# RWKV scan with rate and write keys on 128 rows, and outputs one step behind

## What is computed

```python
def step(S, inp):
    r_t, w_t, k_t, v_t, kk_t, b_t = inp
    sa = jnp.einsum('bhvk,bhk->bhv', S, kk_t)
    S = S * w_t[:, :, None, :] - sa[..., None] * b_t[:, :, None, :] + v_t[..., None] * k_t[:, :, None, :]
    return S, jnp.einsum('bhvk,bhk->bhv', S, r_t)

xs = tuple(jnp.moveaxis(a, 1, 0) for a in (r, w, k, v, kk, b))
S, y = lax.scan(step, s0, xs, reverse=reverse)
```

## Time and profile before

| | us |
|---|---|
| median of 3 runs (lowest, highest) | 1204.44 (1199.67, 1204.90) |
| profiled execution | 1198.73 |
| its span in the trace | 1196.9 |
| PE busy | 1019.0 |
| DVE busy | 420.1 |
| ACT busy | 274.0 |
| POOL busy | 50.1 |
| first diagonal blocks of the scan to its last output | 427.2 to 654.05 |

### The profile page before, as it was taken

One profiled execution on the slowest core, in us unless ns is written; L12 is line 12 of the kernel. 1 busy time (PEld: TensorE's weight loads), 2 busy tenths in 40 slices (PEclk: granted clock), 3 DMA queues, 4 the chain that ended last, 5 costly groups with the idle time before them and its releaser, 6 DMA issues. The chain is left out here.

```text
span 1196.9 us, 22526 instructions
## 1 busy us (share of the span) xinstructions
PE 1019.0 (85%) x9838; PEld 620.8 (52%) x9838; DVE 420.1 (35%) x882; ACT 274.0 (23%) x538; POOL 50.1 (4%) x73
## 2 busy tenths in 40 slices
PE   3699999978777747988899999299999999999970
PEld 0265555544455547887898555244444444444430
DVE  1402642232488753372833664500000000010006
ACT  2311222223676511221122212011111111111101
POOL 0320000010000000000000000300000000000003
PEclk9899999988699877988989999589999999999995
DMA  9713342549998010102101821696899899898907
GB/s 345 236 23 140 120 162 87 196 152 406 407 404 350 10 29 3 39 12 74 47 14 56 316 71 41 239 342 241 318 343 348 306 352 345 311 352 321 331 35 263
DMA packets 95926, 244.95 MB, mean 205 GB/s; under 512 B 6612, under 2 KB 11508, under 8 KB 95328
## 3 DMA queue, kind: packets, MB, share of 16 engines
q1 hardware_dynamic: 85664, 218.64, 50.2%
q10 hardware_dynamic: 5824, 13.69, 2.9%
q0 software_dynamic: 4352, 11.34, 2.9%
HBM read 176.64 MB, written 67.01 MB: 204 GB/s over the span
## 5 line engine op out<-in xcount | busy, mean ns | idle before, releaser
L2091 PE MATMUL ps<-arena 128*128 128x512 f32 x544 | 239.9, 598 | 1.7 <-ACT arena L2141 1.7
L2091 PEld LDWEIGHTS ps<-arena 128*128 128x128 f32 x544 | 102.7, 191 | 127.1 <-issue 126.4
L2105 PE MATMUL ps<-arena 128*128 128x512 f32 x272 | 121.3, 599 | 3.6 <-ACT arena L2145 3.6
L696 PE MATMUL ps<-arena 128*128 128x512 f32 (+3 forms) x448 | 123.6, 435 | 0.0
L696 PEld LDWEIGHTS ps<-arena 128*128 128x128 f32 (+1 forms) x448 | 67.7, 188 | 60.2 <-issue 59.4
L2105 PEld LDWEIGHTS ps<-arena 128*128 128x128 f32 x272 | 50.6, 191 | 62.1 <-issue 62.1
L1760 PE MATMUL ps<-arena 128*128 128x512 f32 x160 | 70.6, 593 | 1.0 <-PEq L1237 1.0
L563 DVE SCALAR_TENSOR_TENSOR arena<-arena 128x128 f32<-128x128 f32 (+3 forms) x56 | 30.9, 552 | 82.6 <-ACT arena L440 81.1
L2182 DVE TENSOR_TENSOR arena<-arena,ps 128x512 f32<-128x512 f32 x17 | 11.7, 689 | 136.8 <-ACT arena L2137 136.8
L2190 DVE COPY arena<-ps 128x512 f32<-128x512 f32 x17 | 11.8, 693 | 125.9 <-PE ps L2105 125.9
L630 PE MATMUL ps<-arena 128*128 128x512 f32 (+1 forms) x160 | 52.4, 485 | 0.0
(11 more groups left out here) (307 smaller groups left out, 1385.3 us busy)
## 6 DMA issues: line engine op xcount, KB each, us to landing
gathered_tokens<-arena SPq DMA_DIRECT2D x16, 2560.0 KB, 26.0
arena<-in_exp_up_dram SPq DMA_DIRECT2D x17, 2048.0 KB, 18.2
arena<-in_exp_gate_dram SPq DMA_DIRECT2D x17, 2048.0 KB, 13.2
arena<-in_exp_down_dram SPq DMA_DIRECT2D x17, 2048.0 KB, 9.8
arena<-in_w_mod_dram SPq DMA_DIRECT2D x12, 2048.0 KB, 13.7
arena<-gathered_tokens SPq DMA_DIRECT2D x18, 512.0 KB, 15.1
expert_outputs<-arena ACTq DMA_DIRECT2D x17, 512.0 KB, 8.1
arena<-in_w_in_dram SPq DMA_DIRECT2D x4, 2048.0 KB, 7.8
```

The costliest lines, as they stand in the source:

```text
L696: mm = pe.matmul(ps[0:m, b, 0:hi - lo], ring[:, slot_of(what), k, (e % 4) * P:(e % 4) * P + m], hT[:, k, lo:hi], start=(k == 0), stop=(k = ...
L2091: mm = pe.matmul(ps[:, b, :], xgT[:, k, :], w[u][:, k, :], start=(k == 0), stop=(k == KT - 1))
L2105: mm = pe.matmul(ps[:, Y0 + half, :], hidT[:, k, :], wd[u][:, k, half * 512:(half + 1) * 512], start=(k == 0), stop=(k == 3))
```

## The change

Four things change in the scan.

First, the tile form. The pair of heads no longer gives the two halves of the rows of a tile; the direction or the kind of key does. A gram product takes the B and K keys of a head together as 128 stationary columns (for z = 1 in the order K, B, by place_of), and A and R as 128 moving ones, and writes 128 rows: one masked tile G takes the place of LR and MR, with one mask operation of 1024 columns per direction. turn_kb becomes 4 transposes per direction. UV holds for each direction the values in one half of the rows and the solved U in the other, so that one product over 128 rows does what two over 64 rows did; the state is kept as a block diagonal of 128 by 128 for each pair of heads. Right sides, solve products and outputs of both directions share one bank and one semaphore.

Second, the values. They are brought into UV by four DMAs a step on POOL's queue, and POOL clears the half in which U will stand, two steps ahead of use at the earliest (UV is double).

Third, the order. outputs(s) moves from behind new_states(s) to behind right_sides(s + 1). First visits of a chunk are copied to ytok by ScalarE, second ones added by VectorE.

Fourth, the output stage turns with 4 transposes of 128 columns where it had 16 products of 64.

The diff, cut:

```diff
+        def place_of(z, k):
+            return 5 - k if z and k >= B_ else k
...
+        G = [place_tile(2, 2 * NC4, 2 * C) for _ in range(2)]
+        KB = [place_tile(2, NC4, P) for _ in range(2)]
+        UV = [place_tile(2, NHEAD, C) for _ in range(2)]
...
+                for s in range(STEPS):
+                    if s >= 2:
+                        pool.wait_ge(y_mm, s - 1)
+                    u = UV[s % 2]
+                    for z in range(2):
+                        for p in range(2):
+                            pool.dma_start(rows(u, 1 - z)[:, z].rearrange("q (j p) n -> q j p n", p=2)[:, :, p, :],
+                                           rows(vt, p)[:, chunk_at(z, s)]).then_inc(ld_v[s % 2], 16)
+                    for z in range(2):
+                        if s or z:
+                            pool.wait_ge(u_zero, 2 * s + z)
+                        pool.memset(rows(u, z)[:, z], 0.0).then_inc(u_zero, 1)
...
+                def gram(s, z):
+                    for j in range(NC4):
+                        for p in range(2):
+                            mm = pe.matmul(ps[:, 2 * z + p, j * P:(j + 1) * P], both(rows(chm, p), z, s, j, B_), both(rows(chm, p), z, s, j, A_),
+                                           start=True, stop=True)
+                    mm.then_inc(g_mm[z], 1)
...
+                            mm = pe.transpose(ps[:, 2 * z, j * P:(j + 1) * P], both(chm, z, s, j, B_), ident)
...
+                    pe.wait_ge(ld_v[s % 2], 64 * (s // 2) + 64)
+                    pe.wait_ge(u_zero, 2 * s + 2)
+                    for j in range(NC4):
+                        if s:
+                            for z in range(2):
+                                pe.matmul(ps[64 * z:64 * z + 64, BRHS, j * P:(j + 1) * P], channels(A_, z, s, j), S[:, z, j],
+                                          start=True, stop=False)
+                        for p in range(2):
+                            for z in range(2):
+                                h = 2 * j + p
+                                mm = pe.matmul(ps[64 * z:64 * z + 64, BRHS, h * C:(h + 1) * C], G[s % 2][:, z, p * NC4 + j, 0:C], u[:, z, h],
+                                               start=(s == 0), stop=(s == 0 or p == 1))
...
+                            mm = pe.matmul(ps[:, BSN + z, j * P:(j + 1) * P], KB[s % 2][:, z, j], pair_of(UV[s % 2][:, z], j),
+                                           start=True, stop=True)
...
                     right_sides(s)
+                    if s:
+                        outputs(s - 1)
...
                         new_states(s)
-                    outputs(s)
-                    if more:
                         inverse(s + 1)
+                outputs(STEPS - 1)
...
+                def masked(s, z):
+                    dve.wait_ge(g_mm[z], s + 1)
+                    if s >= 2:
+                        dve.wait_ge(y_mm, s - 1)
+                    dve.tensor_tensor(G[s % 2][:, z], ps[:, 2 * z:2 * z + 2, :].rearrange("q b (j n) -> q (b j) n", j=NC4),
+                                      mask_s[:, z].unsqueeze(1).to_broadcast([P, 2 * NC4, 2 * C]), ALU.mult).then_inc(g_ok[z], 1)
...
-                for z in range(2):
-                    act.wait_ge(d2_mm[z], s + 1)
-                    act.activation(Uc[:, z], quarter(BSER + z), ACT.Copy).then_inc(uc_ok[z], 1)
+                    act.wait_ge(d2_mm, s + 1)
+                    act.activation(all_heads(rows(UV[s % 2], 0)[:, 0]), rows(ps, 0)[:, BRHS, :], ACT.Copy).then_inc(u_ok[0], 1)
...
+                    dve.wait_ge(d2_mm, s + 1)
+                    dve.tensor_copy(rows(UV[s % 2], 1)[:, 1], rows(ps, 1)[:, BRHS, :].rearrange("q (h n) -> q h n", n=C)).then_inc(u_ok[1], 1)
+                    if s:
+                        second_outputs(s - 1)
...
-                        for cc in range(2):
-                            for p in range(2):
-                                mm = pe.matmul(ps[64 * p:64 * p + 64, tt % 2, c4 * P + cc * C:c4 * P + (cc + 1) * C],
-                                               rows(yn[:, 2 * tt + cc, c4], p), rows(istack, p), start=True, stop=True)
+                        mm = pe.transpose(ps[:, tt % 2, c4 * P:(c4 + 1) * P], heads[:, c4 * P:(c4 + 1) * P], ident)
```

More of the change, by code:

```diff
@@ L82, in const_table @@
     near = ((s // 32 == t // 32) & (s // 16 != t // 16)).astype(np.float32)[:, None]
-    put("mask_b", np.stack([later * (cross - near), incl], 2))
-    put("mask_k", np.stack([later, incl], 2))
+    own = (half[:, None] == np.arange(2)[None])[:, :, None, None]
+    put("mask_s", np.where(own, np.stack([later * (cross - near), incl], 2), np.stack([later, incl], 2)))
     put("eye32", (q % 32)[:, None] == np.arange(32)[None])
@@ L1275, in diag_blocks @@
                     mm.then_inc(m_mm, 1)
-                def gram(s, k, bank, done):
-                    for z in range(2):
-                        for j in range(NC4):
-                            for p in range(2):
-                                q = 64 * half(z, p)
-                                mm = pe.matmul(ps[q:q + 64, bank + z, j * 2 * C:(j + 1) * 2 * C], kinds(k, z, s, j, p),
-                                               kinds(A_, z, s, j, p, 2), start=True, stop=True)
-                        mm.then_inc(done[z], 1)
+                def gram(s, z):
[4 more added lines that the diff above has]
+                    mm.then_inc(g_mm[z], 1)
@@ L1286, in turn_kb @@
                 def turn_kb(s):
                     for z in range(2):
[L1288 removed]
+                        pe.wait_ge(g_ok[z], s + 1)
                         for j in range(NC4):
[L1290 to L1294 removed]
@@ new lines, in right_sides, with by_inverse @@
+                    mm.then_inc(rhs_mm, 1)
+                def by_inverse(s, second, src, done):
+                    for j in range(NC4):
+                        for p in range(2):
+                            h = 2 * j + p
+                            for z in range(2):
+                                b = 1 - FIRST[z] if second else FIRST[z]
+                                q = 64 * z + 32 * b
+                                mm = pe.matmul(ps[q:q + 32, BRHS, h * C:(h + 1) * C], block32(XTf[s % 2], z, b)[:, p * NC4 + j],
+                                               block32(src, z, b)[:, h], start=True, stop=True)
+                    mm.then_inc(done, 1)
@@ L1400, in turned_states @@
+                    mm.then_inc(y_mm, 1)
+                def turned_states(bank, part_of, done):
                     for z in range(2):
```

406 lines of the change are left out of this document (196 added, 210 removed).

## The result

| | before | after |
|---|---|---|
| median (lowest, highest; 13 runs each, same chip) | 1202.78 (1197.22, 1210.96) | 1193.97 (1187.80, 1199.45) |
| profiled execution | 1198.73 | 1191.26 |
| its span in the trace | 1196.9 | 1189.5 |
| scan: first inverse copied out to the end of the last output | 457.52 to 654.05 = 196.5 | 460.30 to 649.28 = 189.0 |

The ratio of after to before is 0.9926, with a 95% interval of 0.9901 to 0.9951: the change gains 0.7%, some 9 us, where I had forecast 21. The time lies inside my wide range (1169 to 1202), 10 us above the forecast of 1184. The direction was right; the size was not.

The account below looks back on a forecast made before the run. TensorE's own instructions bound steady steps; clock loss, diagonal blocks, an issue gap and VectorE add elsewhere. Scan gain 19.0, less 0.5, plus 2.5 makes 21.0 us: from 1204.44 to 1183.4, forecast 1184, likely 1174 to 1190, wide range 1169 to 1202.

Parts of the forecast that it names:

- TensorE's own work in a step: Steady scan step: records times price per tile form sum to 12.6 us, 4.1 us a step less than before.
- step 9: Last scan step: two outputs in it and nothing to hide the copies, 11.6 to 11.9 us against 9.3, loss 2.6.
- the issue gap of step 4: Scan step 4: TensorE gaps of 3.4 and 1.1 us kept as before, in a step of 23.3 us.
- sign that I had named as proof against me: Scan: forecast wrong if PEclk is below 0.9 in steps 7 and 8, or steps 2 and 5 exceed 21 us.
- the first rival: Right sides and outputs: weight loads of column tiles follow one another, 0.7 us more each, 1197 us in all; chance 0.13.
- The waits: Steady step: inner products wait 0.6 us for VectorE's mask, next right sides 1.2 for its state update; step 14.45 us.
- a rival for the clock in steady steps: TensorE's clock falls in steps 2, 5, 7, 8 and 9 too, 10 us in all, 1194 us; chance 0.14.
- Steps 3 and 6: Scan: last row-solve piece, masks, products and update 19.1 us, about 2 of half clock: 21.1, gains 1.8 and 1.9.
- The values on POOL: Four DMAs and two memsets a step on POOL: 10.7 us against a need at 14.45, free with 3.7 to spare.
- The rival for slower: Right sides wait for POOL's value DMAs; at 10 us of landing 26 us more, 1209 us; chance 0.08.
- More is saved: Fewer records and denser tiles spare steps 1, 3, 4 and 6 their half clock: up to 1172 us; chance 0.10.
- Around the scan: Outside the scan: masks and copies before the solve lose 0.5 us, fewer transposes in the output stage gain 2.5.

Follow-up runs that it names:

- outputs_at_end: The changed kernel with each step's outputs put back behind its own new states and inverse; 1182.95 us, ratio 0.9849 to the kernel before.
- filled_last_step: outputs_at_end plus four unused 128x256 Matmuls in the waits of step 9; 1179.51 us, ratio 0.9791 to the kernel before.

## Why the prediction was right or wrong

The mechanism was right and sizes were off. Three terms of the sum failed: TensorE's own work in a step, put at 12.6 us and 13.9 in the trace; step 9, put at 11.9 and 17.2; and the issue gap of step 4, carried over from the kernel before, which grew from 3.4 to 6.4. Neither sign that I had named as proof against me came (PEclk is 1.00 in steps 7 and 8; steps 2 and 5 take 17.8 and 18.65 us). And errors cancelled: step 3 came 1.65 us over and step 2 1.9 under.

**TensorE in a steady step: right in kind, too small by 1.3 us.** The column tiles of the right sides load beside each other: 24 Matmuls in 1.83 us, forecast 1.8, and 2.5 under the first rival. That rival rested on a rule of the Trainium skill, TensorE: Matmul & The Clock Gate, Part 3 (The mechanism), that a weight load overlaps only when its row group differs; here both column tiles use all rows and the rows of the trace show the overlap, so the measurement decides against it for this form. The step's sum of 12.6 was mis-sized: TensorE's own work is 13.9 (13.8 in outputs_at_end). There are two reasons. I had multiplied records by their price and left out the end of each row: the next row of another form begins nearly where the row ends, so a gram takes 1.09 us from start to start for my 1.0, the new states 1.9 for 1.7, the outputs 1.94 for 1.8. More than half of the miss is in the 32-row work, 5.1 us for my 4.4, and there the row itself is longer: 32 records of the form of L1353 take 1.10 us, and 1.03 to the next start, where the earlier trace rows has 0.91 and 0.83. The price was no constant of the form in the kernel before either; in its step 9 the same instructions take longer:

```profile
647.15 1.19 PE L1353 MATMUL ps<-arena 32*32 32x64 f32 x32
```

I took the price from the one place where the row stands behind a long gram. What sets it is not shown.

**The waits: right.** I named a wait of 1.2 us of the right sides for L1643 and of 0.6 for the mask; the trace has 0.8 to 1.5 and 0.35. I also wrote that they arise because the outputs stand behind the right sides, and outputs_at_end confirms it. The steady step came to 15.7 instead of 14.7: 1.3 us more of TensorE's own work, and waits that are 0.3 us shorter together.

**Step 9: the largest miss, 5.3 us.** I listed its parts at full clock and took PEclk 1.00 from before, where only one wait, of 0.2 us, stood in the step. Two things failed. The wait of outputs(9) for the second outputs of step 8 in the one bank `BY`, 2.32 us where I had 0.7 for the copy, was in the code and not in my list. And the new idle time between the products brings the half clock: filling it gave 3.1 us in filled_last_step. In the changed kernel itself the rows at half clock, from 640.6 to 647.5 us, cost some 2.1 us (outputs 3.5 for 1.9, the last product 1.7 for 1.1). I had also left out the wait of the step's right sides, 0.8. I had a rival for the clock in steady steps, where it didn't fall, and none for the last step, where TensorE waits most.

**Step 4: 3.1 us.** I carried the issue gaps over from the earlier trace rows, 3.4 and 1.1 us. They are no constant: one gap of 6.4 stands in their place, 1.9 more, and it lasts until the next packet of instructions has come through beside the load. The other 1.3 us are TensorE's own work, as in every step; the lost clock was as I had it (3.3 us for 3.5).

**Steps 3 and 6: 1.65 and 1.2 us over.** The last piece of the row solve and the masks are as computed; 2 us for the half clock was a little short. The clock was at 0.50 for some 7 us of step 3 and 10 of step 6, and in step 3 the three rows that ran in that stretch took 6.3 us for 3.8. Another 0.9 us of step 3 is where the step is cut: at its start VectorE still has 1.7 us of the last state update to do, at its end 0.8, and step 2 is shorter by the same. Steps 2 and 5 came 1.9 under and 0.25 over, steps 0 and 1 0.9 over and 0.8 under.

**The values on POOL: never waited for.** In the stretch from 600 to 640 us they landed 4.2 us after their issue, and one issue took 617 ns, where I had bounds of 3.1 and 960. Beside the load of w_out in step 4 they took 8.5 us, and still nothing waited. The rival for slower falls. The Trainium skill, SBUF — State Buffer (the "DVE blocks DMA" trap), speaks of VectorE operations that hold up GpSimd's descriptors; nothing of it is seen here beside VectorE's fp32 work of 7.6 us a step, which is masks, additions and scalings, and copies out of PSUM.

**More is saved: did not come.** The half clock of steps 1, 3, 4 and 6 is still there (PEclk 0.74 in step 4).

**Around the scan:** the output stage as forecast; the loss ahead of the scan 0.7 us more than forecast, with 1.6 us in untouched code. The first inverse is copied out between 456.0 and 462.6 us in the kernels of this study, so a single profile can't tell this much.

## What to carry to other kernels

When a change joins work that was staggered, list the waits of the first and the last step of the loop by themselves: there nothing covers them, and idle time there costs the clock too. Work that fills a wait by chance (here the outputs beside the state update) should only be moved if its new place has idle time to give; moving it cost 0.8%, more than half of the 1.5% that the rest of the change had brought. A gap called "issue" beside a large load is no property of the instructions in it: look at when the packets of the instruction queue come, and cut the load into pieces, so that none has to wait for the whole of it. A price read from one row holds for the place of that row; before it is multiplied by the steps, look for the same form in a second place.

## What the runs showed that I had not expected

- TensorE stood for 3.4 to 6.4 us for want of instructions while a load of 2 MB kept the DMA engines busy for 10 to 12 us, in diagonal blocks, grams or transposes alike. The instruction queue (q8) brought no packet for 7.9 to 11.7 us then, and each gap ended 1.4 to 1.5 us behind the landing of the next. In four pieces of 512 KB, no gap.
- Four Matmuls more made a kernel 0.6% faster (0.9849 to 0.9791), through the clock of one stretch; eight larger ones elsewhere, 7.4 us in all, made no difference.
- Two 64-column tiles over all 128 rows run beside each other: 16 records of 128 columns and 32 of 64 in 1.83 us.
